# Interleaving x's high and low parts in the mixer phases of a twelve-phase trunk

## What is computed

```python
for i in range(DEPTH):                                   # 4 layers
    x = x + 0.5 * _swiglu(_rms_norm(x, norm_ffn1[i]), w_gate, w_up, w_down)
    h = _rms_norm(x, norm_mix[i])
    y = (_fox_mixer, _conv_module, _diff_mixer)[i % 3](h, ...)
    x = x + y
    x = x + 0.5 * _swiglu(_rms_norm(x, norm_ffn2[i]), ...)
```

## Time and profile before

| | |
|---|---|
| two timed runs | 1986.12 and 1989.1, median 1987.61 |
| the profiled execution | span 1984.6, from the first to the last instruction; no other time was recorded for it |
| TensorE matmul | busy 1955.5 (99%), 12574 matmuls |
| TensorE weight load | busy 1717.6 (87%) |
| VectorE | busy 1420.7 (72%) |
| ScalarE | busy 1044.4 (53%) |
| GpSimd | busy 101.6 (5%) |
| DMA | 350.14 MB, mean 176 GB/s |
| granted TensorE clock | mean 0.997 of full speed |

### The profile page before, as it was taken

One profiled execution on the slowest core, in us unless ns is written; L12 is line 12 of the kernel. 1 busy time (PEld: TensorE's weight loads), 2 busy tenths in 40 slices (PEclk: granted clock), 3 DMA queues, 4 the chain that ended last, 5 costly groups with the idle time before them and its releaser, 6 DMA issues.

```text
span 1984.6 us, 29082 instructions
## 1 busy us (share of the span) xinstructions
PE 1955.5 (99%) x12574; PEld 1717.6 (87%) x12574; DVE 1420.7 (72%) x1645; ACT 1044.4 (53%) x1250; POOL 101.6 (5%) x114
## 2 busy tenths in 40 slices
PE   7999999999999998999999999999999999999999
PEld 6888889888888896988888888788888888888887
DVE  7776678875787565877587658887758765778763
ACT  6554566554555344654465455575436544566542
POOL 3000001000200001100100000010000000001000
PEclk9999999999999998999999999999999999999999
DMA  7655434655665683665656553356566655435653
GB/s 238 194 183 182 149 128 154 192 188 189 192 191 180 201 249 83 191 191 182 200 191 192 177 184 128 107 176 191 183 196 190 191 183 180 148 128 171 191 189 107
DMA packets 336365, 350.14 MB, mean 176 GB/s; under 512 B 10077, under 2 KB 331886, under 8 KB 336238
## 3 DMA queue, kind: packets, MB, share of 16 engines
q1 hardware_dynamic: 331742, 343.58, 54.1%
q10 hardware_dynamic: 4496, 4.70, 1.2%
HBM read 346.04 MB, written 2.22 MB: 175 GB/s over the span
## 4 chain that ended last, share of the span: by engine, by line
PE 94%; DVE 3%; ACT 2%; issue 1%; POOL 1%; DMA 0%; ACTq 0%; DVEq 0%; POOLq 0%
PE banks L1443 49%; PE banks L1448 24%; PE banks L1434 5%; PE banks L1436 5%; PE banks L1435 5%; PE banks L1901 1%; PE banks L1660 1%; PE banks L1713 1%; ACT sb_w_high L470 1%; DVE sb_w_low L808 1%; PE banks L1680 1%; PE banks L1697 1%; ACT sb_scores L598 0%; PE banks L1818 0%; PE banks L1667 0%
## 5 line engine op out<-in xcount | busy, mean ns | idle before, releaser
L808 DVE TENSOR_TENSOR sb_w_low<-sb_raw,sb_w_high 128x2048 fp32r<-128x2048 f32 (+1 forms) x332 | 749.5, 2262 | 208.8 <-ACT sb_w_high L470 208.2
L1443 PE MATMUL banks<-sb_x_both,sb_w_high 128*128 128x512 f32 x2816 | 721.9, 393 | 1.9 <-ACT sb_w_high L470 1.9
L470 ACT ACTIVATE sb_w_high<-sb_raw 128x2048 fp32r<-128x2048 f32 (+1 forms) x332 | 618.5, 1867 | 122.2 <-DMA sb_raw<-in_ffn_w_down 109.0
L1443 PEld LDWEIGHTS banks<-sb_x_both,sb_w_high 128*128 128x128 f32 x2816 | 500.2, 189 | 82.2 <-ACT sb_w_high L470 2.3
L1448 PEld LDWEIGHTS banks<-sb_x_both,sb_w_low 128*128 128x128 f32 x2792 | 386.5, 188 | 35.2
L1448 PE MATMUL banks<-sb_x_both,sb_w_low 128*128 128x256 f32 x2792 | 394.6, 279 | 0.0
L1443 PE MATMUL banks<-sb_h_both,sb_w_high 128*128 128x512 f32 x1408 | 360.2, 395 | 0.0
L1443 PEld LDWEIGHTS banks<-sb_h_both,sb_w_high 128*128 128x128 f32 x1408 | 250.8, 188 | 45.3
L1448 PEld LDWEIGHTS banks<-sb_h_both,sb_w_low 128*128 128x128 f32 x1408 | 190.9, 188 | 16.9
L1448 PE MATMUL banks<-sb_h_both,sb_w_low 128*128 128x256 f32 x1408 | 194.4, 279 | 0.0
L488 ACT ACTIVATE sb_x_both<-sb_xT,sb_vec 128x256 fp32r<-128x256 f32 x96 | 43.3, 501 | 200.8 <-DVE sb_xT L841 176.1
(11 more groups left out here) (229 smaller groups left out, 1936.6 us busy)
## 6 DMA issues: line engine op xcount, KB each, us to landing
sb_raw<-in_ffn_w_gate SPq DMA_DIRECT2D x88, 1024.0 KB, 5.4
sb_raw<-in_ffn_w_up SPq DMA_DIRECT2D x88, 1024.0 KB, 5.3
sb_raw<-in_ffn_w_down SPq DMA_DIRECT2D x64, 1024.0 KB, 5.0
sb_raw<-in_ffn_w_down SPq DMA_DIRECT2D x32, 768.0 KB, 4.3
sb_raw<-in_fox_w_in SPq DMA_DIRECT2D x24, 1024.0 KB, 5.2
sb_raw<-in_conv_w_pw SPq DMA_DIRECT2D x12, 1024.0 KB, 5.4
sb_raw<-in_diff_w_in SPq DMA_DIRECT2D x12, 1024.0 KB, 5.0
sb_raw<-in_fox_w_out SPq DMA_DIRECT2D x8, 1024.0 KB, 4.8
```

The costliest lines, as they stand in the source:

```text
L470: act.activation(slot(w_high, b)[:, 0:width(b)], slot(raw, b)[:, 0:width(b)], ACT.Copy).then_inc(S["high_ready"], 1)
L808: dve.tensor_tensor(slot(w_low, b)[:, 0:width(b)], slot(raw, b)[:, 0:width(b)], slot(w_high, b)[:, 0:width(b)].bitcast(F32), ALU.subtract) ...
L1443: return pe.matmul(pair(bank[at][:, :]), high[:, n * P:(n + 1) * P], m_both, start=first, stop=last, skip_group_check=True)
```

## The change

`x_both` becomes one flat row with 256 floats to spare. A table gives for each mixer phase the place where x begins in it and whether the parts are paired. Paired means that element n of a tile's high part and element n of its low part are neighbours: a tile takes 2048 bytes, and each part is read and written with a step of 8 bytes. The feed-forward phases keep the old order at place 16, which is the old address (the 16 floats of `shift_x` are gone). `h_both` keeps its order and has a place of 216 floats, in the room of `shift_h`'s 200.

```diff
+X_PLACE = {1: (16, True), 4: (0, True), 7: (32, True), 10: (0, True)}
...
-        sb("shift_x", [P, 16])
-        x_both = sb("x_both", [P, 2, KT, SEQ], F32R)
-        x_high, x_low = x_both[:, 0, :, :], x_both[:, 1, :, :]
+        x_both = sb("x_both", [P, 2 * KT * SEQ + 256], F32R)
...
-        sb("shift_h", [P, 200])
...
-            h_both = during_ffn.enter_context(nc.sbuf_tensor("sb_h_both", [P, 2, FF_TILES, SEQ], F32R))
+            h_both = during_ffn.enter_context(nc.sbuf_tensor("sb_h_both", [P, 2 * FF_TILES * SEQ + 256], F32R))
...
+        def parts(buf, place, tiles):
+
+            at, paired = place
+            flat = buf[:, at:at + 2 * tiles * SEQ]
+            if paired:
+                return flat.rearrange("p (k n a) -> p a k n", a=2, n=SEQ)
+            return flat.rearrange("p (a k n) -> p a k n", a=2, n=SEQ)
+
+        def x_parts(i):
+            return parts(x_both, X_PLACE.get(i, (16, False)), KT)
+
+        def h_parts(i):
+            return parts(h_both, (216, False), FF_TILES)
...
-                    act.activation(x_high[:, t, :], xT[:, t, :], ACT.Copy, scale=vec[:, col + t:col + t + 1]
+                    act.activation(x_parts(i)[:, 0, t, :], xT[:, t, :], ACT.Copy, scale=vec[:, col + t:col + t + 1]
...
-                    dve.scalar_tensor_tensor(x_low[:, t, :], xT[:, t, :], vec[:, col + t:col + t + 1],
-                                             x_high[:, t, :].bitcast(F32), ALU.mult, ALU.subtract
+                    dve.scalar_tensor_tensor(x_parts(i)[:, 1, t, :], xT[:, t, :], vec[:, col + t:col + t + 1],
+                                             x_parts(i)[:, 0, t, :].bitcast(F32), ALU.mult, ALU.subtract
...
-                                       x_high[:, k, :], x_low[:, k, :], k == 0, k == KT - 1)
+                                       x_parts(i)[:, 0, k, :], x_parts(i)[:, 1, k, :], k == 0, k == KT - 1)
...
-                    ins = three_passes(dst[:, tt * 256:(tt + 1) * 256], x_high[:, k, toks], x_low[:, k, toks],
+                    ins = three_passes(dst[:, tt * 256:(tt + 1) * 256], x_parts(i)[:, 0, k, toks],
+                                       x_parts(i)[:, 1, k, toks],
```

More of the change, by code:

```diff
@@ L242, in pair, with x_wide, h_wide @@
             return t.rearrange("p (a n) -> p a n", a=2)
+        def parts(buf, place, tiles):
[8 more added lines that the diff above has]
+            return parts(h_both, (216, False), FF_TILES)
+        def x_wide(i, k):
+            return x_parts(i)[:, :, k, :]
+        def h_wide(i, k):
+            return h_parts(i)[:, :, k, :]
         def over_tokens(row, n=2):
@@ L551, in high @@
                     act.wait_ge(S["hidden_ready"], PAIRS * f + p + 1)
-                    act.activation(h_both[:, 0, 2 * p:2 * p + 2, :], pair(hidden[:, :]), ACT.Copy
+                    act.activation(h_parts(i)[:, 0, 2 * p:2 * p + 2, :], pair(hidden[:, :]), ACT.Copy
                                    ).then_inc(S["h_high_ready"], 1)
@@ L982, in low @@
                     dve.wait_ge(S["h_high_ready"], PAIRS * f + p + 1)
-                    dve.tensor_tensor(h_both[:, 1, 2 * p:2 * p + 2, :], pair(hidden[:, :]),
-                                      h_both[:, 0, 2 * p:2 * p + 2, :].bitcast(F32),
+                    dve.tensor_tensor(h_parts(i)[:, 1, 2 * p:2 * p + 2, :], pair(hidden[:, :]),
+                                      h_parts(i)[:, 0, 2 * p:2 * p + 2, :].bitcast(F32),
                                       ALU.subtract).then_inc(S["h_low_ready"], 1)
@@ L1449, in on_high, with both_parts @@
                           start=False, stop=False, skip_group_check=True)
-            def both_parts(at, n, high, low, m_both, ks, first, last):
+            def both_parts(at, n, high, low, m_both, m_high, ks, first, last):
                 for k in ks[:1]:
@@ L1456, in both_parts @@
                 for k in ks:
-                    on_high(at, n, low[:, k, :], m_both(k)[:, 0, :])
+                    on_high(at, n, low[:, k, :], m_high(k))
                 for k in ks[1 if first else 0:]:
@@ L1460, in both_parts, with columns_half @@
                 return ins
-            def columns_half(dst, b, n, tiles=range(KT)):
+            def columns_half(i, dst, b, n, tiles=range(KT)):
                 high, low = (slot(t, b).rearrange("p (k n) -> p k n", k=KT) for t in (w_high, w_low))
@@ L1467, in columns_half, with tokens_half @@
                     ins = three_passes(dst[:, n * SEQ:(n + 1) * SEQ], high[:, k, cols], low[:, k, cols],
-                                       x_high[:, k, :], x_low[:, k, :], k == 0, k == KT - 1)
+                                       x_parts(i)[:, 0, k, :], x_parts(i)[:, 1, k, :], k == 0, k == KT - 1)
                 return ins
-            def tokens_half(dst, b, tt, tiles=range(KT)):
+            def tokens_half(i, dst, b, tt, tiles=range(KT)):
                 high, low = (slot(t, b).rearrange("p (k n) -> p k n", k=KT) for t in (w_high, w_low))
@@ L1516, in first_block @@
                         ins = three_passes(dst[:, n * SEQ:(n + 1) * SEQ], high[:, k, cols], low[:, k, cols],
-                                           x_high[:, k, :], x_low[:, k, :], k == 0 and n == 0, k == KT - 1, True)
+                                           x_parts(i)[:, 0, k, :], x_parts(i)[:, 1, k, :], k == 0 and n == 0,
+                                           k == KT - 1, True)
                 ins.then_inc(S["block_done"], 1)
@@ L1556, in tile @@
                     high, low = (slot(t, blk).rearrange("p (k n) -> p k n", k=KT) for t in (w_high, w_low))
-                    return both_parts(pair_banks(p) + 2 * which + n, n, high, low, lambda k: x_both[:, :, k, :],
-                                      list(ks), ks[0] == 0, ks[-1] == KT - 1)
+                    return both_parts(pair_banks(p) + 2 * which + n, n, high, low, lambda k: x_wide(i, k),
+                                      lambda k: x_parts(i)[:, 0, k, :], list(ks), ks[0] == 0, ks[-1] == KT - 1)
                 def very_first_pair():
@@ L1569, in very_first_pair @@
                                 for n in range(2):
-                                    on_both(at + n, n, high[:, k, :], x_both[:, :, k, :], k == 0, False)
+                                    on_both(at + n, n, high[:, k, :], x_wide(i, k), k == 0, False)
                             if which == 0 and ks[0] == 0:
@@ L1574, in very_first_pair @@
                                     for k in ks:
-                                        on_high(at + n, n, low[:, k, :], x_high[:, k, :])
+                                        on_high(at + n, n, low[:, k, :], x_parts(i)[:, 0, k, :])
                         wait_block(which)
@@ L1579, in very_first_pair @@
                                 ins = pe.matmul(bank[at + n][:, SEQ:2 * SEQ], low[:, k, n * P:(n + 1) * P],
-                                                x_high[:, k, :], start=False, stop=k == KT - 1, skip_group_check=True)
+                                                x_parts(i)[:, 0, k, :], start=False, stop=k == KT - 1, skip_group_check=True)
                         ins.then_inc(S["block_done"], 1)
@@ L1616, in down @@
                     for n in range(2):
-                        ins = both_parts(2 * (T % 2) + n, n, high, low, lambda k: h_both[:, :, first + k, :],
+                        ins = both_parts(2 * (T % 2) + n, n, high, low, lambda k: h_wide(i, first + k),
+                                         lambda k: h_parts(i)[:, 0, first + k, :],
                                          list(range(last - first)), c == 0, c == len(DOWN) - 1)
@@ L1730, in fox_group @@
                         wait_block(q_blk)
-                        columns_half(bank[0], q_blk, 0)
-                        columns_half(bank[0], q_blk, 1).then_inc(S["block_done"], 1)
+                        columns_half(i, bank[0], q_blk, 0)
+                        columns_half(i, bank[0], q_blk, 1).then_inc(S["block_done"], 1)
                         score_pair(0, g, u)
@@ L1737, in fox_group @@
                     wait_block(k_blk)
-                    columns_half(bank[1], k_blk, 0)
-                    columns_half(bank[1], k_blk, 1).then_inc(S["block_done"], 1)
+                    columns_half(i, bank[1], k_blk, 0)
+                    columns_half(i, bank[1], k_blk, 1).then_inc(S["block_done"], 1)
                     if j:
@@ L1748, in fox_group @@
                         pe.wait_ge(S["v_ready"], 4 * a + j + u)
-                    tokens_half(bank[2], v_blk, 0, range(3))
+                    tokens_half(i, bank[2], v_blk, 0, range(3))
                     if j:
                         score_pair(1, g, u)
-                    tokens_half(bank[2], v_blk, 0, range(3, KT))
+                    tokens_half(i, bank[2], v_blk, 0, range(3, KT))
                     if j:
@@ L1757, in fox_group @@
                         head_sums("k", j, u)
-                    tokens_half(bank[2], v_blk, 1, range(2))
+                    tokens_half(i, bank[2], v_blk, 1, range(2))
```

(18 more changed lines are left out.)

2 lines of the change are left out of this document (1 added, 1 removed).

## The result

The changed kernel takes 2156.03 us (two runs, 2154.72 and 2157.34) against 1987.61. The ratio is 1.0847, with a 95% interval of 1.0815 to 1.0878. The forecast was 1981 with a range of 1966 to 2004. It was wrong, and in sign too.

What follows compares the result with a forecast made beforehand. TensorE's step from matmul to matmul was taken to bound the kernel. 1984.6 - 6.4 = 1978.2 us profiled, with 3.0 added for timed runs, gave 1981 us; own range 1974 to 1988, full range 1966 to 2004.

Steps and rivals of the forecast that it cites:

- What bounds the kernel: Whole kernel: TensorE is nearly always busy, so a change of the step between matmuls goes straight into the span.
- The strided moving operand: q, k and conv blocks, also v's term: -4.5 ns for each matmul now slow, together -6.4 us.
- The count of 1536: Matmuls in the mixers that get a moving operand with a step of 8 bytes, 3 x 512.
- The bounds: Price of the strided stream: from -20 us, all excess gone, to +154 us, half rate as in the transposes.
- Nearest row: Basis for the price between the ends: the same instruction's own fast step, 113.3 ns against 117.8.
- The rule weighed beside it: Strided reads of x: two hits on a 16-byte line suffice, so the term is 0 or a gain.
- Rival 3, half rate: Column matmuls: a step of 8 bytes halves the stream, +154 us, 2142 us, up to 2183 with v's loads; chance 0.10.
- Rival 2, price by lines passed: q, k and conv blocks: the excess of 6.6 to 11.1 ns is paid twice, +15 us, 2003 us; chance 0.16.
- The strided stationary operand: v's weight loads with a step: costed at nothing, at most +41 us for 384 loads, with half rate only.
- the cover: v's weight loads: the 113 ns of the matmul beside each load, expected to hide it.
- The writes: ScalarE's x_high and VectorE's x_low tiles, written with the step: costed at nothing, at most +3 us in all.
- The moved tensors: h_both moved 1024 bytes, o_high and o_low 160: taken as zero, bounded by 5 us and 3 us either way.

Runs made afterwards that it cites:

- the unpaired kernel: The changed kernel with the pairing alone taken out, new places and moved tensors kept: 1992.75 us, ratio 1.0028 to the kernel before.
- the one with old places: The changed kernel without pairs, x at place 16 in every phase, o_high 512 bytes on from its old address: 1987.90 us, ratio 1.000.

## Why the prediction was wrong

- **What bounds the kernel**: right. TensorE was busy throughout, and a change of its step went into the span one for one, but for the 5 us that diff's waits absorbed.
- **The strided moving operand**: this is the step that failed. The count of 1536 was right; the price was put at the matmul's own fast step, -4.5 ns where it was slow, and it measured +109 ns in conv (226.7 against 117.8; 2.2 ns of it are the place). The bounds held the danger (217 ns from the transposes). The choice between the ends was poor. "Nearest row" was taken as the same instruction; but the property that the change touches, how a line's floats are used by the stream, was the same in every row of before, so none of them was near. The steps of 113 and 118 ns and the difference of x and h told of places, and I let a few ns of placement stand for the price of a pattern.
- **The rule weighed beside it.** The Trainium skill (Advanced Engine Details and Errata, SBUF Cachelines) asks for at least two hits on a 16-byte line to absorb the access latency, and the prediction took two as enough. The moving stream disagrees: two hits run at 226.7 ns, four at 117.8. The stationary load agrees: two hits 195 ns against 189, one hit 328. The measurement decides, separately for the two operands.
- **Rival 3, half rate**: this is what happened. It gave 2142 us. The 14 us missing are 9 of price (163 us for pairing instead of 154, with 226.7 instead of 217 ns a step and a part of it absorbed in diff) and the 4.9 us of the places. It had a chance of 0.10, which was too little for a price that no row showed. With its own sum standing at 2142, a range that stopped at 2004 rested on that chance alone.
- **Rival 2, price by lines passed**: its price of 6.6 to 11.1 ns was a tenth of the 109 ns measured or less, and a price for the bytes covered is refuted for the moving stream. Aligned runs of four cover the same 2048 bytes as pairs at 117.8 ns, and steps of 16 and 32 bytes, which cover two and four times as many, differ from pairs by +6.6 and -8.9 ns.
- **The strided stationary operand at nothing**: right within 1.4 us for all of v; with 16 bytes the cover was gone. The prediction's count was wrong: it took 384 of v's loads as strided, but all three loads of a triple read x, 576 in all, so its upper bound should have been 62 us instead of 41. The step of 16 bytes measured 58 us on v's matmuls (133.6 - 75.6).
- **The writes at nothing**: right. The two x_low tiles before phase 1 take 0.89 us instead of 0.88, ScalarE's write of a tile 514 to 524 ns instead of some 502, and no wait of TensorE for them appeared.

```profile
205.56 0.89 DVE L871 SCALAR_TENSOR_TENSOR sb_x_both<-sb_xT,sb_vec,sb_x_both 128x256 fp32r<-128x256 f32 x2 [0.59 <-ACT sb_x_both L507]
```

- **The moved tensors at nothing**: right for h (1.86 us still). For `o_high` wrong by what the bound allowed: by the sum of its starts the output projection takes 94.0 us in the unpaired kernel against 90.9, at a step of 120.0 ns that is neither of the prediction's two. Together with x's new places it is the 4.9 us between the unpaired kernel and the one with old places.

## What to carry to other kernels

An operand's layout has a price of its own even where it changes no byte count and no instruction: before interleaving two arrays that TensorE streams, check whether each 16-byte line that is touched is used up by the one stream. If two parts must be interleaved, alternate them in aligned runs of four float32, which cost nothing here (one run, in conv alone). And where a trace has no row with the property that a change introduces, the nearest row in kind says little about it; take the chance of the bad bound seriously, or measure one phase first.

## What the runs showed of the hardware

For 256 float32 columns (read as fp32r, clock granted in full), step from one matmul to the next:

| moving operand | floats used of a line | ns |
|---|---|---|
| contiguous, ten places | 4 | 113 to 122 |
| runs of four, aligned | 4 of every other line | 118 |
| step of 8 bytes | 2 | 227 |
| runs of two, 8 bytes apart | 2 | 227 |
| runs of four across two lines | 2 and 2 | 233 |
| step of 16 bytes | 1 | 233 |
| step of 32 bytes | 1 of every other line | 218 |

The other accesses to x go by another condition: with two floats of a line they are nearly as fast as with four, and with one they take 1.4 to 1.8 times as long. In ns, for 128 columns loaded as weights, and for one tile of 256 floats in the mixer phases (VectorE also reads x_high with the step):

| | contiguous | step of 8 bytes | 16 bytes | 32 bytes |
|---|---|---|---|---|
| weight load | 189 | 195 | 328 | 336 |
| ScalarE writes x_high | 502 to 504 | 514 to 524 | 743 to 744 | 766 to 770 |
| VectorE writes x_low | 483 to 485 | 485 to 487 | 701 to 708 | 747 to 754 |

A line of three used floats and other types were not tried, and why the 32-byte step is 15 ns faster than 16 is open. A place alone moves the step by up to 8 ns: conv's first block goes at 113.3 ns with x at 16, 119.9 at 0 and 121.0 at 18. By what rule it does is left open.
